# Writing out the 24 passes of a scan on three engines, and spreading a side computation over other stages

## What is computed

```python
def ada_modulation(cond, w, b):                 # for the first block and for each of four layers
    m = jax.nn.silu(cond) @ w + b
    shift, scale, gate = jnp.split(m, 3, axis=-1)
...
def sgu_mixer(h, w_in, gain, w_s, b_s, w_out):
    u, v, z = jnp.split(h @ w_in, 3, axis=-1)
    u = jax.nn.gelu(u)
    v = rms_norm(jax.nn.gelu(v), gain)
    mixed = jnp.einsum('gpq,bcqgd->bcpgd', w_s, vc) + b_s.T[:, :, None]
    s = u * mixed.reshape(bsz, length, SGU_WIDTH)
    return (s * jax.nn.silu(z)) @ w_out
...
    def step(S, inp):                           # rwkv7_scan: 16 heads, two directions, 768 tokens
        s_kk = jnp.einsum('nbhvk,nbhk->nbhv', S, kk_t)
        S = S * w_t[..., None, :] - s_kk[..., :, None] * (kk_t * a_t)[..., None, :] + v_t[..., :, None] * k_t[..., None, :]
        y_t = jnp.einsum('nbhvk,nbhk->nbhv', S, inp[5]) if emit else None
```

## Time and profile before

| what | us |
|---|---|
| three runs | 6240.05, 6240.1, 6243.55 (median 6240.1) |
| the profiled execution | 6241.25 |
| its span (first to last instruction) | 6239.7 |
| TensorE busy in it | 5428.0 (87%) |
| VectorE busy | 2470.2 (40%) |
| ScalarE busy | 1210.1 (19%) |
| GpSimd busy | 423.9 (7%) |

### The profile page before, as it was taken

One profiled execution on the slowest core, in us unless ns is written; L12 is line 12 of the kernel. 1 busy time (PEld: TensorE's weight loads), 2 busy tenths in 40 slices (PEclk: granted clock), 3 DMA queues, 4 the chain that ended last, 5 costly groups with the idle time before them and its releaser, 6 DMA issues.

```text
span 6239.7 us, 91668 instructions
## 1 busy us (share of the span) xinstructions
PE 5428.0 (87%) x36014; PEld 3148.1 (50%) x36014; DVE 2470.2 (40%) x4422; ACT 1210.1 (19%) x1968; POOL 423.9 (7%) x397
## 2 busy tenths in 40 slices
PE   7977878898999799997983489889688999999999
PEld 3556545543444345554551388888443444444443
DVE  2348543455234411104109666666613454511110
ACT  2113222300220111101016200000112333310120
POOL 0014200000000000000005200000100000000000
PEclk9989988899999899998995699999899999999999
DMA  3311310153224211111224411111110000011121
GB/s 133 102 65 61 108 70 20 43 177 124 69 80 150 90 38 43 50 47 38 88 105 177 143 37 37 38 37 37 49 44 33 22 16 22 12 61 68 65 72 74
DMA packets 92937, 428.58 MB, mean 69 GB/s; under 512 B 9953, under 2 KB 10081, under 8 KB 75105
## 3 DMA queue, kind: packets, MB, share of 16 engines
q1 hardware_dynamic: 71072, 338.34, 15.6%
q0 software_dynamic: 21568, 85.99, 4.1%
HBM read 364.53 MB, written 59.77 MB: 68 GB/s over the span
## 4 chain that ended last, share of the span: by engine, by line
PE 71%; issue 8%; DVE 7%; PEld 5%; DVEq 4%; DMA 2%; ACT 2%; PEldq 0%; POOLq 0%; POOL 0%; ACTq 0%; SPq 0%
PE psum L371 42%; PE psum L2664 12%; PE psum L2244 6%; PEld psum L371 4%; PE psum L1970 2%; PE psum L1969 2%; PE psum L633 1%; PE psum L1992 1%; DVEq L2521 1%; DVEq L2531 1%; PE psum L1014 1%; DVE sbuf L648 1%; PE psum L1259 1%; DVE sbuf L2942 1%; DVE sbuf L1373 1%
## 5 line engine op out<-in xcount | busy, mean ns | idle before, releaser
L371 PE MATMUL psum<-sbuf 128*128 128x512 f32 (+4 forms) x8640 | 3218.1, 533 | 216.2 <-DVEq L1479 66.9
L371 PEld LDWEIGHTS psum<-sbuf 128*128 128x128 f32 (+1 forms) x8640 | 1575.3, 192 | 1824.7 <-issue 1586.8
L2664 PE MATMUL psum<-sbuf 64*64 64x64 f32 (+1 forms) x21504 | 807.9, 230 | 137.0 <-issue 72.8
L2664 PEld LDWEIGHTS psum<-sbuf 64*64 64x64 f32 x21504 | 772.2, 136 | 173.3 <-issue 161.8
L2244 PE MATMUL psum<-sbuf 128*128 128x512 f32 (+1 forms) x1088 | 358.0, 490 | 30.9 <-DVE sbuf L2224 29.1
L2244 PEld LDWEIGHTS psum<-sbuf 128*128 128x128 f32 x1088 | 207.3, 191 | 181.6 <-issue 163.8
L1487 DVE SCALAR_TENSOR_TENSOR sbuf<-psum,sbuf 128x512 f32 x64 | 42.3, 682 | 562.4 <-PE psum L371 562.4
L2758 ACT ACTIVATE sbuf<-psum 128x256 f32<-128x256 f32 x192 | 76.1, 438 | 856.8 <-PE psum L2664 855.5
L2428 PE MATMUL psum<-sbuf 64*128 64x512 f32 (+2 forms) x192 | 91.6, 738 | 145.7 <-ACT sbuf L2482 68.2
L1761 DVE SCALAR_TENSOR_TENSOR sbuf<-psum,sbuf 128x512 f32<-128x512 f32 (+1 forms) x48 | 30.3, 659 | 456.6 <-PEq L1728 456.6
L616 ACT ACTIVATE sbuf<-sbuf 128x512 f32<-128x512 f32 (+1 forms) x114 | 52.9, 552 | 674.9 <-DVEq L2985 660.5
(11 more groups left out here) (274 smaller groups left out, 4833.3 us busy)
## 6 DMA issues: line engine op xcount, KB each, us to landing
sbuf<-w_side POOLq DMA_DIRECT2D x128, 512.0 KB, 3.9
sbuf<-w_sgu_uz SPq DMA_DIRECT2D x32, 1088.0 KB, 5.0
sbuf<-terms SPq DMA_DIRECT2D x120, 256.0 KB, 2.7
sbuf<-w_up SPq DMA_DIRECT2D x22, 1024.0 KB, 4.9
sbuf<-w_merge SPq DMA_DIRECT2D x8, 2560.0 KB, 8.9
sbuf<-w_sgu_v SPq DMA_DIRECT2D x8, 2048.0 KB, 8.2
sbuf<-w_sgu_out SPq DMA_DIRECT2D x16, 1024.0 KB, 4.7
terms<-sbuf SPq DMA_DIRECT2D x8, 1920.0 KB, 11.3
```

The source lines that it names most:

```text
L371: last = nc.tensor.matmul(out, w, x, start=(n == 0), stop=(n == len(pairs) - 1))
L2664: last = t.matmul(out[hs], lhs[hs], rhs[hs], start=start, stop=stop)
```

## The change

It has two parts.

**The scan.** `passes` gets a flag with which the 21 passes of the loop are written out one after the other; TensorE, VectorE and ScalarE use it. The values of waits and the addresses become constants. The semaphore `passed` and its increments are gone, and a wait of TensorE is a plain wait. SP keeps its loop.

**The side work.** `GateZ` has two later blocks for u = 1 where it had one. `Merge` has one later block for each tile where it had seven. The `Residual` of `w_down` has none. `SguMix` of layer 0 is now host 3, with four later blocks for u = 0 and five for u = 1 over 8 turns; its side results go to a spare stretch of SBUF. There the conditions are fetched at the start of the stage, Silu comes behind ScalarE's first square root, and GpSimd issues the loads of a tile behind the scaling of the tile after it. The order of the blocks is the same, and the 24 later blocks that layer 0 needs are made in `GateZ` and `Merge`.

```diff
-    HOSTS = [(((0,), (1,)), KX // 2, ("first", "first")), (((0,), (1,)), KS // 2, ("first", "later")),
-             (((0, 1, 0, 1, 0, 1, 0), (1, 0, 1, 0, 1, 0, 1)), KD // 2, ("later", "later")),
-             (((0, 1, 0, 1), (0, 1, 0, 1)), KD // 2, ("later", "later"))]
+    HOSTS = [(((0,), (1,)), KX // 2, ("first", "first")), (((0,), (1, 0)), KS // 2, ("first", "later")),
+             (((0,), (1,)), KD // 2, ("later", "later")),
+             (((0, 1, 0, 1), (0, 1, 0, 1, 0)), KG // 2, ("later", "later"))]
...
 class SguMix(Stage):
     def gpsimd(self, pool):
+        if self.side:
+            self.side.rows_of(pool)
         pool.wait_ge(self.inverted, 1)
 
-        def body(i, u):
+        def stage(i, u):
             pool.wait_ge(self.gated, 2 * i + u + 1)
             self.nc.gpsimd.tensor_tensor(self.staged_v[u], one(self.v, 2 * i + u), over(self.inv, P), ALU.mult
                                          ).then_inc(self.staged, 1)
-        pairs(pool, KG, body)
+
+        def load(i, u):
+            if self.side:
+                self.side.load(pool, 3, i, u)
+
+        stage(0, 0)
+        with pool.Fori(0, KG // 2 - 1) as i:
+            stage(i, 1)
+            load(i, 0)
+            stage(i + 1, 0)
+            load(i, 1)
+        stage(KG // 2 - 1, 1)
+        load(KG // 2 - 1, 0)
+        load(KG // 2 - 1, 1)
...
     def scalar(self, act):
         a.activation(self.total, self.total, ACT.Sqrt, scale=1.0 / SGU_W, bias=EPS).then_inc(self.rooted, 1)
+        if self.side:
+            self.side.silu(act, 3)
...
     def vector(self, dve):
         dve.sem_inc(self.gated, 2)
+        if self.side:
+            self.side.start(dve, 3)
...
             v.tensor_tensor(one(self.s, 2 * i + u), self.tmp[u], self.z[u], ALU.mult).then_inc(self.gated, 1)
+            if self.side:
+                self.side.reduce(dve, 3, i, u, self.junk)
...
-    def passes(self, eng, make, alone):
-
-        make(0, 0, 0, None)
-        with eng.Fori(0, KD - 1) as m:
+    def passes(self, eng, make, alone, written_out=False):
+
+        def pair(m):
             for b in range(BATCHES):
                 make(3 * m + b + 1, m + (b + 1) // BATCHES, (b + 1) % BATCHES, (3 * m + b, m, b))
+
+        make(0, 0, 0, None)
+        if written_out:
+            for m in range(KD - 1):
+                pair(m)
+        else:
+            with eng.Fori(0, KD - 1) as m:
+                pair(m)
...
-        def wait(sem, value):
-
-            pe.wait_ge(sem, value)
-            pe.sem_inc(self.passed, 1)
-
+        wait = pe.wait_ge
...
-        self.passes(pe, make, alone)
+        self.passes(pe, make, alone, written_out=True)
```

More of the change, by code:

```diff
@@ L1603, in block1 @@
         FfnUp(chip),
-        Residual(chip, "w_down", KF, lambda k: g[:, k], part(5, 0), side=side),
+        Residual(chip, "w_down", KF, lambda k: g[:, k], part(5, 0)),
         Norm(chip, "norm_out", [dict(x=x_lat, out=x_lat, gain=chip.vec("final_g"))], A_WORK),
@@ L2771, in make @@
                 copy(self.w[d], self.slots(d, 2, 2)).then_inc(self.w_out[d], 1)
-        self.passes(act, make, nothing)
+        self.passes(act, make, nothing, written_out=True)
     def vector(self, dve):
@@ L2858, in alone @@
                 step(*past, s)
[L2859 removed]
+        self.passes(dve, make, alone, written_out=True)
 class RwkvOutput(Stage):
```

38 lines of the change are left out of this document (14 added, 24 removed).

## The result

| | before | after |
|---|---|---|
| median of 4 runs each, same chip | 6240.08 us | 6086.47 us |
| lowest and highest of after | | 6084.52 to 6103.35 us |
| ratio, 95% interval | | 0.9757, 0.9744 to 0.9771 |
| profiled execution, its span | 6241.25, 6239.7 us | 6084.52, 6082.9 us |

Two executions of later kernels, 13821.53 and 10835.84 us, ran at a mean granted clock of 0.54 and 0.56 and are left out of every median.

The account below looks back on a forecast made before the run. The prediction took TensorE, with 71% of the chain that ended last, to bound the kernel. From 6241.25 us it took 49 (returns), 22 (increments) and 11.5 (side work), giving 6158.8, as a median 6157 us; whole range 6128 to 6185.

Parts of the forecast that it names:

- What bounds the kernel: Whole kernel: TensorE holds 71% of the chain that ended last; an edit pays only where it takes idle time off TensorE.
- First term: Scan loop: six returns to the loop's head cost about 8.1 us each; writing out saves 49 us, bounds 44 and 52.
- rival D: Scan: a return's cost is TensorE waiting for the clearing of states and the terms, which stay; 6206 us, chance 0.05.
- Second term: TensorE's scan program: 1416 increments of 51 ns leave, saving 22 us, bounds 6 and 72.
- then a stretch costs 4.38 us whatever is in it: Scan's narrow matmuls: pauses are waits for the next 16 KB of program, so fewer instructions mean more matmuls per stretch.
- the lower bound: Scan: 0.10 us saved at each release where TensorE waits for VectorE, some 60 in the scan, 6 us.
- rival B: Scan: the increments lie on the path in whole, 72 us, giving 6107 us; chance 0.08.
- the 10.97 us stretch: Scan, where the program runs straight on: 224 matmul records from one pass into the next, without a break.
- Constants and registers: Scan passes: constants in place of register instructions save 0, up to 0.3 us a pass where the compared passes don't show it.
- Side work: Merge -21.4, w_down -15.1, GateZ +3.6, SguMix's end +17.4 and start +4: sum -11.5 us, bounds -16 and -8.
- Rival C: SguMix: VectorE becomes the bound, from 3.9 us a block; at 4.2, 22 us more, 6179 us; chance 0.07.
- Rival E: Scan's narrow part: VectorE's and ScalarE's program fetches come between TensorE's and lengthen its pauses; slower, 6270 us; chance 0.04.

## Why the prediction was wrong, and where it was right

**What bounds the kernel** was right in the main: everything was gained on TensorE. But "takes idle time off TensorE, and nowhere else" is too narrow, for 50.5 of the scan's 128.8 us are TensorE's busy time.

**First term, six returns, -49.** Right in mechanism and nearly in size. Before to everything written out with increments is 918.5 - 864.0 = 54.5 us (60.1 from the 924.1 of the other kernel with the old scan), somewhat above the bound of 52. That TensorE's return is not a wait for the clearing or the terms (rival D) is shown by the passes with clearing, 31.6 us like the rest. The clock has a share: in the kernel before, windows at the return of the earlier trace rows:

```profile
3674.00:3678.00 4.00, 2.41 (x44) 1.00 0.02 4
3678.00:3682.00 4.00, 0.44 (x4) 0.76 0.29 78
3682.00:3686.00 4.00, 3.65 (x40) 0.50 0.46 131
3686.00:3690.00 4.00, 3.84 (x90) 0.89 0.26 66
```

After 2.96 and 2.55 us of idle time the clock is at its lower level of 1.2 GHz for all of 3682 to 3686. That is why the piece of 124 records took 7.49 us where 6.07 was its share; I had counted these 1.4 us without naming their cause. In the windows of 20 us at the six returns the shortfalls of the clock add up to 1.02 x 20 = 20 us, the most that the clock can have in the 54.5. The price of 108 ns that the Trainium skill gives for a compare-and-branch ("Advanced Engine Details and Errata", Control Flow Timing) is not the price of a return here: TensorE's branch lasts 83 ns where it leaves the loop and 3.3 to 3.8 us where it goes back, and the whole return costs 9.3 us for TensorE's alone.

**Second term, increments, -22, bounds 6 and 72.** This is the step that failed; it measured 74.3, above even its upper bound, and this difference of 52 us is most of the miss. The failed sentence is "then a stretch costs 4.38 us whatever is in it". I read the even spacing of the earlier trace rows as a fixed time for 16 KB of program, so that fewer instructions could only lengthen the stretches. The number of packets did fall much as reckoned (page: 222 to 204 in the whole run, 16 KB each as before), but the pauses themselves went, from 72.8 us to 1.1. A stretch has no fixed time: with fewer semaphore instructions of 51 ns between the products its pause vanishes, and the products themselves take less of TensorE's busy time (785.7 to 757.4 us).

The count was wrong as well. Not 1416 instructions leave with the increments but 912, because an increment and its wait were one instruction and 504 waits stay as instructions of their own. So the bound of 72, all at 51 ns, should have been 46.5, and the measured 74.3 lies far above it. The chain of after still has 0.14 us behind a release at some waits (3666.19) and 0.04 at others (3667.48), so the 0.10 us of the lower bound didn't come at each release either. The argument against rival B, "the 10.97 us stretch runs without a break with as many increments in it", proved too much: those are the wide products, and even there 60 increments a pass cost 39.5 us, 24.4 of them as busy time of TensorE (781.8 against 757.4) and the rest as idle time. In rival B the size was near, 72 against 74.3, but by luck: it is 1416 times 51 ns where 912 instructions left. Its total of 6107 would have been 20 us off. That a crossing is mostly hidden, the rule of "Runtime: NRT & Kernel Launch" (Instruction fetch mechanics) in the Trainium skill, agrees with after, where TensorE pauses 1.1 us in all over nearly as many packets of 16 KB (204; 208 with the increments back). If the pauses are crossings, it doesn't hold with the increments in the program, 40.3 us in 65 pauses. That the pauses are fetches of program and that a head start of the sequencer hides them is argued from this and from their multiples of some 124 records, not shown: no run changed the fetch alone.

**What is left open** is why the increments cost 35 us more in all behind the waits than ahead of them, why semaphore instructions cost here and register instructions don't, and why 61 among the narrow products bring longer pauses than 122.

**Constants and registers, 0.** Right. The passes that follow no return are equal with TensorE's register instructions and without, 34.56 and 34.58 us. The sum of the measured terms, 54.5 + 74.3 = 128.8, is the whole change of the scan by construction.

**Side work, -11.5.** It measured -15.4: Merge -21.3 (-21.4), w_down -15.1 (-15.1), GateZ +4.2 (+3.6), SguMix +16.8 (+21.4). In SguMix the term too large is the start, for which I took 4 us. TensorE's wait for its first weights grew from 10.36 us to 10.95, 0.6 us:

```profile
2271.11 2.04 PE L1722 MATMUL psum<-sbuf 128*128 128x128 f32 x8 [10.95 <-DMA sbuf<-w_sgu_uz]
```

Rival C doesn't come in: the stage is longer by its tail and start alone. The stretching that it asked about is there. GpSimd's scaling and VectorE's sums do hold each other up:

```profile
2608.89 1.23 DVE L583 CUSTOM_DVE_ANT_0 sbuf<-sbuf 128x1024 f32<-128x1024 f32 x1 [0.21 <-DMA sbuf<-w_side]
...
2609.31 2.13 POOL L1696 TENSOR_TENSOR sbuf<-sbuf 128x768 f32<-128x768 f32 x1
...
2610.24 2.29 DVE L583 CUSTOM_DVE_ANT_0 sbuf<-sbuf 128x1024 f32<-128x1024 f32 x1
...
2613.21 1.23 DVE L583 CUSTOM_DVE_ANT_0 sbuf<-sbuf 128x1024 f32<-128x1024 f32 x1 [0.21 <-issue]
```

```profile
L1696 POOL TENSOR_TENSOR sbuf<-sbuf x32: 1040/1252/2411, 2266.6 to 5931.0; 128x768 f32<-128x768 f32 x16, 128x512 f32<-128x512 f32 x16
```

One sum took 2.29 instead of 1.23 us, the scaling that it overlaps 2.13, and GpSimd's longest scaling 2411 ns where it was 1468. The exclusive lock of the Trainium skill ("SBUF — State Buffer", SBUF: two separate sides) would look like this. By it, as an estimate from these rows, the scaling would wait for the first sum, 2610.12 - 2609.31 = 0.81 us, and last 0.81 + 1.25 = 2.06. The second sum would wait until 2611.44 and last 1.20 + 1.23 = 2.43. The rows have 2.13 and 2.29. VectorE's slack took it in, as forecast.

**Rival E, slower through more fetching,** has nothing for it: with VectorE and ScalarE written out too, TensorE's pauses went.

**The sum.** The forecast was 82.5 us off the profiled execution, the measurement 156.7. Of the 74 between them the increments are 52.3, the returns 5.5, the side work 3.9, and 12.5 lie in stages that the diff doesn't touch. Of these the 2.1 of the norm come with the change, and much of the rest is chance: the stage of 104.7 us before and 99.8 after ran from 98.4 to 105.1 us in other kernels with the same code for it.

## What to carry to other kernels

On a stretch of many short products, count TensorE's sequencer as an engine of its own. Each semaphore instruction that was added to its program here, an increment or a wait that doesn't go along with a product, cost between 28 and 123 ns where its row says 51, partly as later pauses without a releaser and partly as longer busy time. Count instructions in the page and the source view, not lines of the kernel: a wait can cost none, and a wait with an increment one. When pauses are evenly spaced, don't take the spacing for a fixed time: ask which work would have to be shorter for them to vanish, and keep the upper bound in the range until a run has excluded it. Writing a loop out pays in full only if all engines that meet in it are written out, since one engine's return costs nearly as much as all of them.

## What the runs showed of the hardware

- A wait as an instruction of the sequencer takes 51 ns like an increment, and writing all 1416 waits twice cost 40 us of 790, with nothing more to wait for.
- An increment behind a wait shares its instruction: 1416 of each are 1416 instructions. Without increments 504 of the 1416 waits are instructions and the rest go along with a product.
- With 912 more instructions in either kernel, increments behind the waits cost about twice as much as ahead of them, +74.3 against +38.9 us. 462 register instructions cost nothing that shows.
- TensorE's compare-and-branch lasts 83 ns where it leaves the loop and 3.3 to 3.8 us where it goes back.
- Each return of the loop drops TensorE's granted clock to its lower level for a few microseconds (0.50 in 3682 to 3686, behind 2.96 and 2.55 us of idle time); so does a pause of 2.11 us in the middle of the scan (0.57 in the next 4 us). After has neither, and its scan runs at 1.00 throughout 3600 to 4200.
- Twice the increments can be a little faster: 122 a pass gave 943.3 us of scan, 61 gave 954.5, of which the clock has up to 35.
